# First mixer: level 0's masked copies ahead of the rotations, and two groups of TensorE's order exchanged

## Chip, cores and metric

One core of a Trainium2 chip. The metric is device time in microseconds (us). The kernel runs two transformer layers on 256 tokens of width 1024 in float32.

## What is computed

Layer 0 is a mixer followed by a mixture of experts; layer 1 is another mixer followed by another mixture of experts. The change lies in the mixer of layer 0. There one projection feeds two parts whose outputs are concatenated and projected back:

```python
def even_mixer(h, w_in, lb, hg_norm, q_norm, k_norm, w_out, pos):
    proj = h @ w_in
    hq, hf, hi, hg, aq, ak, av, iq, ik, iw = jnp.split(proj, ...)
    o_h = hgrn2_scan(hq, kk, hi, log f)          # 4 heads of 128, chunks of 64
    o_h = rmsnorm(o_h) * silu(hg)
    q, k = rope(rmsnorm(aq)), rope(rmsnorm(ak))  # 8 query heads, 2 key heads of 64
    o_a = dsa_attention(q, k, v, iq, ik, iw)     # top 64 keys by an index score, softmax
    return concat(o_h, o_a) @ w_out
```

The scan is a gated linear recurrence. The attention takes, for each query, the 64 keys with the highest index score among those of its own and earlier chunks.

## The kernel before

The tokens are two blocks of 128 (t = 0, 1). The projection's weights lie in HBM as units of at most 2 MB; SP loads them into a ring of seven slots in SBUF. The units of layer 0's mixer are, in order, index queries, forget gates, keys and values, queries, scan queries, scan inputs (unit 5) and output gates (unit 6). Units 5 and 6 are multiplied in halves: `half (5, 0)` is unit 5 for tokens 0 to 127, 16 matmuls into PSUM bank 2, and `half (5, 1)` the other 128 tokens, into bank 3; unit 6 follows in the same banks.

The scan is worked out as a masked product of decayed queries and keys, put together from nine levels. Level 0 is the diagonal. For each other level, GpSimd subtracts cumulated decays (L1218, L1219), ScalarE takes exponentials (`level` on ScalarE, L1008), VectorE multiplies them into keys and queries (`mix`, L1420 and L1421), TensorE makes 16 products (`level`, L558 and L561; 8 at level 8), and VectorE copies the part that the level's mask selects into the matrix `aT` (`take_level`, L1406). The products of levels 0 to 5 go to banks 0 and 1, so TensorE may start level v only when level v-1 has been taken (semaphore `lv_ok`).

The attention runs beside it. VectorE picks the 64 keys (`keys`), normalizes queries and keys (`norms`, L1361) and rotates them (`rotate`, L1380, which calls `rope`, L1308, once for each block of tokens; six instructions, L1314 to L1319). TensorE transposes the rotated heads (`turned`, L438), and ScalarE copies them out of PSUM (L999). Then come three batches, each with the same steps: TensorE's `score` (L521), VectorE's masked maximum (`score`, L1429), ScalarE's exponentials (`score`, L1015), TensorE's transposes (`turn`, L530), ScalarE's copies (`turn`, L1021), TensorE's `value` (L540), VectorE's division (`value`, L1441).

Each engine runs these pieces in an order that is written out by hand in three lists at the top of the file, `PE_ORDER` (L59), `DVE_ORDER` (L62) and `ACT_ORDER` (L66); a loop at the end of each engine's part (L575, L1451, L1027) calls the pieces in that order. An engine takes its instructions in order, so a piece that waits for a semaphore holds up everything behind it in its list. GpSimd works through the levels in order; it writes level v's differences when VectorE has mixed level v-2.

Behind the lists come the last products of the scan (L572), the out projection in two halves (L598), and the normalization of the scan's output on VectorE, whose last instructions (L1464) raise `on_ok`. TensorE's second part of the out projection waits for it, and so does SP: the first loads of expert weights into the extra buffers (L379, issued at L341) wait for `on_ok`. The expert weights of a layer are eight groups of twelve units of 2 MB. SP's queue is in order too: five units go into ring slots as the mixer's units leave them (slot of unit 6 after `half (6, 1)`), then come the extra buffers, then everything else.

A piece's waits are its first lines, as here for TensorE's and ScalarE's part of one batch of attention:

```python
def turn(b):                                  # TensorE
    pe.wait_ge(at_exp, b + 1)                 # ScalarE's exponentials of batch b
    ...
def value(b):                                 # TensorE
    pe.wait_ge(at_t, 2 * (b + 1))             # ScalarE's two copies of the turned batch
    ...
def half_unit(which):                         # TensorE
    ...
        pe.wait_ge(e_half, t + 1)             # unit 6: unit 5's copy out of the same bank
```

Of the kernel before, what the change touches and what calls it, by code (L numbers as in the profile page):

```python
# [55 lines left out]

BATCHES = [(0, list(range(8))), (1, [0, 1, 4, 5]), (1, [2, 3, 6, 7])]

PE_ORDER = [("half", (5, 0)), ("level", 0), ("half", (5, 1)), ("level", 1), ("turned", 0), ("level", 2), ("score", 0), ("half", (6, 0)),  # L59
            ("turn", 0), ("level", 3), ("value", 0), ("score", 1), ("half", (6, 1)), ("turn", 1), ("level", 4), ("value", 1), ("score", 2),  # L60
            ("level", 5), ("level", 6), ("turn", 2), ("level", 7), ("value", 2), ("level", 8)]
DVE_ORDER = [("keys", 0), ("keys", 1), ("norms", 0), ("query", 0), ("mix", 1), ("mix", 2), ("rope", 0), ("level", 0), ("rope", 1),  # L62
             ("level", 1), ("mix", 3), ("level", 2), ("mix", 4), ("score", 0), ("level", 3), ("mix", 5), ("value", 0), ("score", 1),
             ("level", 4), ("mix", 6), ("value", 1), ("score", 2), ("level", 5), ("mix", 7), ("level", 6), ("mix", 8), ("level", 7),
             ("value", 2), ("level", 8), ("sum", 0)]
ACT_ORDER = [("level", 1), ("level", 2), ("queries", 0), ("half", (5, 0)), ("level", 3), ("level", 4), ("half", (5, 1)), ("turned", 0),  # L66
             ("level", 5), ("score", 0), ("level", 6), ("half", (6, 0)), ("turn", 0), ("score", 1), ("level", 7), ("half", (6, 1)),
             ("turn", 1), ("score", 2), ("level", 8), ("turn", 2), ("gate", 0)]

LEVEL_BANK = (0, 0, 0, 0, 0, 0, 2, 0, 2)  # L70
# [28 lines left out]
def build(nc, A, out):  # L99
# [7 lines left out]
    with ctx:  # L107
# [3 lines left out]
        def sem(name):  # L111
            return ctx.enter_context(nc.semaphore(name))
# [157 lines left out]
        rot_ok, rot_ps, rot_t = sem("rot_ok"), sem("rot_ps"), sem("rot_t")  # L270
# [128 lines left out]
        def _(pe):  # L399
# [174 lines left out]

            for kind, n in PE_ORDER:  # L575
                {"level": level, "half": half_unit, "turned": turned, "score": score, "turn": turn, "value": value}[kind](n)
# [362 lines left out]
        def _(act):  # L939
# [86 lines left out]

            for kind, n in ACT_ORDER:  # L1027
                {"level": level, "half": half_unit, "queries": queries, "turned": turned, "score": score, "turn": turn, "gate": gate}[kind](n)
# [195 lines left out]
        def _(dve):  # L1224
# [83 lines left out]
            def rope(t, h0, h1):  # L1308

                n = h1 - h0  # L1310
                a1, a2 = rb[:, t, h0:h1, 0:32], rb[:, t, h0:h1, 32:64]
                cos, sin = bc(cs[:, t:t + 1, 0:32], [P, n, 32]), bc(cs[:, t:t + 1, 32:64], [P, n, 32])
                r = lambda m: rt[:, m, 0:32 * n].rearrange("p (h d) -> p h d", h=n)
                ch.put(tt(r(0), a1, cos, ALU.mult))  # L1314
                ch.put(tt(r(1), a2, sin, ALU.mult))
                ch.put(tt(r(2), a2, cos, ALU.mult))
                ch.link(tt(r(3), a1, sin, ALU.mult))
                ch.link(tt(a1, r(0), r(1), ALU.subtract))
                tt(a2, r(2), r(3), ALU.add).then_inc(rot_ok, 1)  # L1319
# [58 lines left out]
                    ch.link(tt(rb[:, t, 8:10, :], rb[:, t, 8:10, :], bc(qkn[:, 1:2, :], [P, 2, 64]), ALU.mult))  # L1378

            def rotate(t):  # L1380
                rope(t, 0, 10)

            def query(_):
# [66 lines left out]

            for kind, n in DVE_ORDER:  # L1451
                {"level": take_level, "mix": mix, "keys": top_keys, "norms": norms, "rope": rotate, "query": query, "score": score,
                 "value": value, "sum": hgrn_sum}[kind](n)
# [477 lines left out]
```

## Time and profile before

| | |
|---|---|
| time, median of 3 runs | 1262.14 us (1261.61 to 1263.18) |
| profiled execution | 1262.0 us, its span 1260.1 us |
| mean granted TensorE clock | 0.924 of full speed |
| busy: TensorE, VectorE, ScalarE, GpSimd | 79%, 27%, 14%, 1% |
| chain that ended last | DMA 39%, TensorE 35%, SP's queue 16% |
| read from HBM | 457 MB, mean 364 GB/s over the span |

The profile is of one execution. PE is TensorE's matmuls, PEld its weight loads, DVE VectorE, ACT ScalarE, POOL GpSimd, and SPq SP's queue of transfers. Times in a timeline count from the span's start; a line is one instruction or several of the same kind that follow each other, and a bracket at its end tells how long the engine had been idle before it and what it then waited for. The granted clock is TensorE's clock as a share of full speed (1.00 is 2.4 GHz, 0.50 is 1.2 GHz).

### The profile page before, as it was taken

The page shows a single profiled execution, that of the slowest core. Times are in us where ns is not written, and L with a number is a line of the kernel's source. Part 1 is how long each engine was busy: PE and PEld are TensorE (multiplying, and loading weights), DVE is VectorE, ACT ScalarE, POOL GpSimd, SP SyncE. Part 2 cuts the span into 40 slices and gives each one's busy share as a digit, 9 for nine tenths or more (in the row PEclk, how much of TensorE's full clock was granted, in tenths as well). Part 3 has the DMA queues.
Part 4 walks back from the last instruction along what each step waited for, and adds up shares of the span by engine and source line. Part 5 has one row for each costly group of instructions (what it writes and reads, how often), then busy time and mean ns, then how long its engine had stood idle before and what let it go on. Part 6 is the DMA issues. An engine that isn't in the chain of part 4 may idle for free.

```text
span 1260.1 us, 20742 instructions
## 1 busy us (share of the span) xinstructions
PE 1001.1 (79%) x8905; PEld 606.8 (48%) x8905; DVE 334.1 (27%) x992; ACT 178.8 (14%) x393; POOL 18.4 (1%) x20
## 2 busy tenths in 40 slices
PE   9999999757576766667999999999857576666665
PEld 6667466424242424333888775465424242423332
DVE  4895341101010110002747553241101010101001
ACT  2315130000000000001224561030000000000000
POOL 0121000000000000000000000000000000000000
PEclk9999999988887988888999999999979887989889
DMA  9931599999999999999944546679999999999998
GB/s 377 416 135 67 226 400 429 428 427 431 426 430 427 430 427 430 428 428 426 409 171 168 184 151 273 261 294 427 426 430 427 430 427 430 428 430 428 430 426 334
DMA packets 34656, 458.91 MB, mean 364 GB/s; under 512 B 3856, under 2 KB 4656, under 8 KB 7216
## 3 DMA queue, kind: packets, MB, share of 16 engines
q1 hardware_dynamic: 33408, 454.00, 86.2%
q10 hardware_dynamic: 1200, 4.23, 1.0%
q8 instruction: 36, 0.59, 0.2%
q14 instruction: 12, 0.10, 0.0%
HBM read 457.13 MB, written 1.08 MB: 364 GB/s over the span
## 4 chain that ended last, share of the span: by engine, by line
DMA 39%; PE 35%; SPq 16%; DVE 2%; issue 1%; another core or an unknown queue 0%; ACT 0%; DVEq 0%
DMA extra<-in_moe_units 20%; DMA ring<-in_moe_units 19%; SPq L341 16%; PE bank L793 11%; PE bank L685 6%; PE bank L895 4%; PE bank L704 3%; PE bank L598 2%; PE bank L664 1%; PE bank L422 1%; PE bank L716 1%; PE bank L852 1%; PE bank L561 1%; PE bank L643 1%; PE bank L630 1%
## 5 line engine op out<-in xcount | busy, mean ns | idle before, releaser
L685 PE MATMUL bank<-ring,xT 128*32 128x256 f32 x2560 | 185.3, 437 | 83.4 <-DMA ring<-in_moe_units 83.4
L685 PE MATMUL bank<-extra,xT 128*32 128x256 f32 x1536 | 123.5, 475 | 71.8 <-DMA extra<-in_moe_units 71.8
L685 PEld LDWEIGHTS bank<-ring,xT 128*32 128x32 f32 x2560 | 84.4, 119 | 169.1 <-DMA ring<-in_moe_units 96.8
L793 PE MATMUL bank<-h,ring 128*128 128x256 f32 x576 | 130.1, 382 | 0.0
L793 PEld LDWEIGHTS bank<-h,ring 128*128 128x128 f32 x576 | 107.4, 190 | 16.5 <-issue 2.9
L685 PEld LDWEIGHTS bank<-extra,xT 128*32 128x32 f32 x1536 | 53.1, 128 | 128.4 <-DMA extra<-in_moe_units 84.9
L704 PE MATMUL bank<-ring,gates_ 128*32 128x256 f32 x1024 | 73.2, 434 | 42.6 <-DMA ring<-in_moe_units 42.6
L704 PE MATMUL bank<-extra,gates_ 128*32 128x256 f32 x1024 | 71.2, 425 | 35.8 <-DMA extra<-in_moe_units 33.4
L1575 DVE TENSOR_TENSOR hT<-hT,bank 128x128 f32<-128x128 f32 x64 | 18.4, 288 | 254.6 <-ACT hT L1065 254.6
L1065 ACT ACTIVATE hT<-bank 128x128 f32<-128x128 f32 x64 | 17.7, 277 | 449.0 <-PE bank L685 449.0
L716 PE MATMUL bank<-xT,gates_ 128*128 128x256 f32 x256 | 70.2, 407 | 3.8 <-DVE xT L1580 2.2
L704 PEld LDWEIGHTS bank<-ring,gates_ 128*32 128x32 f32 x1024 | 34.0, 121 | 79.4 <-DMA ring<-in_moe_units 56.7
L1577 DVE COPY gates_<-bank 128x128 f32<-128x128 f32 x64 | 18.7, 292 | 190.9 <-PE bank L692 190.9
L704 PEld LDWEIGHTS bank<-extra,gates_ 128*32 128x32 f32 x1024 | 34.3, 119 | 64.3 <-DMA extra<-in_moe_units 41.6
L1580 DVE COPY xT<-bank 128x256 f32<-128x256 f32 x32 | 13.6, 425 | 180.7 <-PE bank L704 180.7
L664 PE MATMUL bank<-hT,xn 128*128 128x128 f32 x512 | 60.4, 276 | 1.0 <-DVE hT L1534 1.0
L716 PEld LDWEIGHTS bank<-xT,gates_ 128*128 128x128 f32 x256 | 45.8, 195 | 31.8 <-issue 21.3
L664 PEld LDWEIGHTS bank<-hT,xn 128*128 128x128 f32 x512 | 59.7, 192 | 2.7 <-issue 2.0
L1483 DVE TENSOR_TENSOR xT<-bank,small 128x512 f32<-128x512 f32 (+1 forms) x36 | 22.8, 633 | 111.6 <-PE bank L664 111.6
L1068 ACT ACTIVATE xT<-bank 128x256 f32<-128x256 f32 x32 | 12.3, 383 | 270.4 <-PE bank L704 270.4
L422 PE MATMUL bank<-ring,hT 128*128 128x512 f32 (+1 forms) x128 | 49.4, 541 | 0.0
L422 PEld LDWEIGHTS bank<-ring,hT 128*128 128x128 f32 x128 | 23.9, 190 | 22.2 <-issue 21.2
(312 smaller groups left out, 899.8 us busy)
## 6 DMA issues: line engine op xcount, KB each, us to landing
ring<-in_moe_units SPq DMA_DIRECT2D x112, 2048.0 KB, 49.1
extra<-in_moe_units SPq DMA_DIRECT2D x80, 2048.0 KB, 49.3
ring<-in_od_in_units SPq DMA_DIRECT2D x10, 2048.0 KB, 32.6
ring<-in_ev_in_units SPq DMA_DIRECT2D x5, 2048.0 KB, 26.5
ring<-in_od_out_units SPq DMA_DIRECT2D x4, 2048.0 KB, 8.1
ring<-in_ev_out_units SPq DMA_DIRECT2D x2, 2048.0 KB, 28.4
hT<-sums ACTq DMA_DIRECT2D x4, 512.0 KB, 4.4
every<-sums ACTq DMA_DIRECT2D x4, 512.0 KB, 5.6
```

The costliest lines, as they stand in the source:

```text
L341: sp.dma_start(moe_memory(layer, u), moew[layer, bass.ds(group, 1), u, :, :].rearrange("g p c -> (g p) c")) \
L422: last = mm(bank[b][:, 0:n], hT[:, k, P * t:P * t + P], w[:, k, :], start=(k == 0), stop=(k == KT - 1))
L598: last = mm(bank[2 * t + h][:, :], hT[:, 4 * OUT_BLOCKS[0][u] + k, P * t:P * t + P], w[:, k, 512 * h:512 * h + 512], start=(u == 0 and k = ...
L664: last = mm(bank[b][:, P * (k - k0):P * (k - k0) + P], xn[:, t, P * k:P * k + P], sel[:, 4 * t:4 * t + 4, :].rearrange("p e c -> p (e c)") ...
L685: last = mm(bank[4 + e % 2][32 * j:32 * j + 32, 0:256], xT[:, 4 * part + k, CAP * e:CAP * e + CAP], w[:, k, :, 256 * (j // 2) + j % 2:256 ...
L704: last = mm(bank[6 + q % 2][32 * e:32 * e + 32, 256 * (q // 2):256 * (q // 2) + 256], heT[:, e, CAP * j:CAP * j + CAP], w[:, e, j, :], sta ...
L716: last = mm(o, pgT[:, t, :], ys[:, 256 * q:256 * q + 256], start=last_quarter, stop=end and q > 0)
L793: last = mm(o, w[:, k, P * q:P * q + P], (h2 if u else hT)[:, k, :], start=(k == 0), stop=(k == KT - 1))
L895: last = mm(bank[4 * (g % 2) + 2 * t + h][:, :], yT(g, k)[:, P * t:P * t + P], w[:, k, 512 * h:512 * h + 512], start=(k == 0), stop=(k == 3))
L1483: tt(xT[:, k0:k0 + n, :], bank[b][:, 0:P * n].rearrange("p (k c) -> p k c", k=n), bc(fg[:, layer, k0:k0 + n].unsqueeze(2), [P, n, P]), ALU ...
L1575: tt(he, sg, bank[4 + e % 2][:, P:2 * P], ALU.mult).then_inc(m["he_ok"], 1)
L1577: v_.tensor_copy(heT[:, e, :], bank[7][:, 0:P]).then_inc(m["ht_ok"], 1)
```

## The change

Three orders change, and one wait is added.

- VectorE: `take_level(0)` goes ahead of `rotate(0)`, so the order is mix 2, take 0, rotation 0, rotation 1, take 1.
- TensorE: `half (6, 0)` moves from behind score 0 to behind level 1, ahead of the transposes (`turned`) and level 2; and level 3 and turn 0 change places. The order is now half (5, 1), level 1, half (6, 0), turned, level 2, score 0, level 3, turn 0, value 0.
- ScalarE: the copy of half (5, 1) goes ahead of the exponentials of levels 3 and 4, and the copy of half (6, 0) goes from behind level 6 to behind the copies of the transposes, ahead of level 5.
- VectorE's second rotation waits for the last instruction of the first, since both use the scratch tile `rt` and the copies of level 0 no longer stand between them.

No instruction is added or removed but that wait, and no transfer changes.

```diff
-PE_ORDER = [("half", (5, 0)), ("level", 0), ("half", (5, 1)), ("level", 1), ("turned", 0), ("level", 2), ("score", 0), ("half", (6, 0)),
-            ("turn", 0), ("level", 3), ("value", 0), ("score", 1), ("half", (6, 1)), ("turn", 1), ("level", 4), ("value", 1), ("score", 2),
+PE_ORDER = [("half", (5, 0)), ("level", 0), ("half", (5, 1)), ("level", 1), ("half", (6, 0)), ("turned", 0), ("level", 2), ("score", 0),
+            ("level", 3), ("turn", 0), ("value", 0), ("score", 1), ("half", (6, 1)), ("turn", 1), ("level", 4), ("value", 1), ("score", 2),
             ("level", 5), ("level", 6), ("turn", 2), ("level", 7), ("value", 2), ("level", 8)]
-DVE_ORDER = [("keys", 0), ("keys", 1), ("norms", 0), ("query", 0), ("mix", 1), ("mix", 2), ("rope", 0), ("level", 0), ("rope", 1),
+DVE_ORDER = [("keys", 0), ("keys", 1), ("norms", 0), ("query", 0), ("mix", 1), ("mix", 2), ("level", 0), ("rope", 0), ("rope", 1),
...
-ACT_ORDER = [("level", 1), ("level", 2), ("queries", 0), ("half", (5, 0)), ("level", 3), ("level", 4), ("half", (5, 1)), ("turned", 0),
-             ("level", 5), ("score", 0), ("level", 6), ("half", (6, 0)), ("turn", 0), ("score", 1), ("level", 7), ("half", (6, 1)),
+ACT_ORDER = [("level", 1), ("level", 2), ("queries", 0), ("half", (5, 0)), ("half", (5, 1)), ("level", 3), ("level", 4), ("turned", 0),
+             ("half", (6, 0)), ("level", 5), ("score", 0), ("level", 6), ("turn", 0), ("score", 1), ("level", 7), ("half", (6, 1)),
...
             def rotate(t):
+                if t:
+                    dve.wait_ge(rot_ok, 3)
                 rope(t, 0, 10)
```

## Rows read from the trace of the kernel before

**Rows 1.** The page's slices of the span, 40 of 31.5 us: DMA busy share.

```profile
DMA  9931599999999999999944546679999999999998
```

**Rows 2.** Timeline of TensorE, 50 to 150 us: start, us, engine, line, operation.

```profile
74.62 1.95 PE L558 MATMUL bank<-extra 128*128 128x128 f32 x16
76.40 7.03 PE L422 MATMUL bank<-ring,hT 128*128 128x512 f32 x16
84.11 2.02 PE L561 MATMUL bank<-xn 128*128 128x128 f32 x16 [0.68 <-DVE aT L1406]
86.80 1.31 PE L438 MATMUL bank<-con,rb 128*128 128x128 f32 x10 [0.67 <-DVE rb L1319]
88.17 2.02 PE L561 MATMUL bank<-xn 128*128 128x128 f32 x16
90.13 1.71 PE L521 MATMUL bank<-tt_ 64*128 64x128 f32 x16
91.77 7.13 PE L422 MATMUL bank<-ring,hT 128*128 128x512 f32 x16
98.74 1.04 PE L530 MATMUL bank<-con,pr 128*128 128x128 f32 x8
99.61 1.95 PE L561 MATMUL bank<-xn 128*128 128x128 f32 x16
101.40 1.90 PE L540 MATMUL bank<-av,rt 128*128 128x64 f32 x16
...
121.11 1.09 PE L530 MATMUL bank<-con,pr 128*128 128x128 f32 x8 [0.45 <-ACT pr L1015]
```

**Rows 3.** SP's timeline, and stretches: length, busy PE, PEld, DVE, ACT, POOL, PEclk, DMA share, GB/s.

```profile
139.22 1.91 SPq L341 DMA_DIRECT2D extra<-in_moe_units  x4
...
131.20:139.20 8.00, 7.15 (x17) 2.98 (x17) 7.33 (x19) 0.00 (x0) 0.00 (x0) 1.00 0.00 0
139.20:150.00 10.80, 10.80 (x32) 5.30 (x33) 0.00 (x0) 1.57 (x4) 0.00 (x0) 1.00 0.91 360
```

**Rows 4.** Timeline of VectorE, 50 to 150 us.

```profile
77.27 1.39 DVE L1314 TENSOR_TENSOR rt<-rb,extra 128x320 f32<-128x320 f32 x1
...
82.64 1.33 DVE L1406 COPY_PREDICATED aT<-extra,bank 128x512 f32<-128x512 int32 x2
84.00 0.49 DVE L1314 TENSOR_TENSOR rt<-rb,extra 128x320 f32<-128x320 f32 x1
...
86.26 0.49 DVE L1319 TENSOR_TENSOR rb<-rt 128x320 f32<-128x320 f32 x1
...
88.06 0.69 DVE L1420 TENSOR_TENSOR xn<-extra,ro 128x512 f32<-128x512 f32 x1
...
90.23 1.34 DVE L1406 COPY_PREDICATED aT<-extra,bank 128x512 f32<-128x512 int32 x2 [0.88 <-PE bank L561]
91.61 0.69 DVE L1420 TENSOR_TENSOR xn<-extra,ro 128x512 f32<-128x512 f32 x1
...
92.82 0.29 DVE L1429 CUSTOM_DVE_ANT_0 pr<-bank,sc 128x128 f32<-128x128 f32 x1
```

**Rows 5.** Timeline of ScalarE, 50 to 150 us.

```profile
87.50 1.36 ACT L999 ACTIVATE tt_<-bank 128x512 f32<-128x512 f32 x3 [3.34 <-PE bank L438]
...
95.08 0.40 ACT L1015 ACTIVATE pr<-pr,sm 128x128 f32<-128x128 f32 x1 [2.29 <-DVE sm L1432]
...
98.17 1.04 ACT L1008 ACTIVATE ro<-ro 128x1024 f32<-128x1024 f32 x1
...
99.69 1.06 ACT L1021 ACTIVATE rt<-bank 128x512 f32<-128x512 f32 x2
```

**Rows 6.** Expert loop: TensorE's timeline, and one stretch (length, PE busy, PEclk, DMA, GB/s).

```profile
252.96 2.02 PE L685 MATMUL bank<-ring,xT 128*32 128x256 f32 x32 [2.79 <-DMA ring<-in_moe_units]
257.86 3.47 PE L685 MATMUL bank<-ring,xT 128*32 128x256 f32 x32 [2.61 <-DMA ring<-in_moe_units]
...
258.00:261.00 3.00, 3.00 (x32) 0.52 0.99 421
```

## The prediction

> **What bounds the kernel now.** I read the page first, then the chain of work that ended last, then the timelines of the first mixer engine by engine. The page's DMA line shows the case's shape: transfers fill the chip for most of the span, with holes in the third and fourth slices, about 63 to 126 us [rows 1]. That hole is the part of the first mixer that the diff touches. The reader should see in TensorE's timeline that from 74.6 us on its groups stand almost shoulder to shoulder [rows 2]: it waits 0.68 us ahead of level 1, 0.67 us ahead of the head transposes ("turned"), and 0.45 us ahead of turn 2. So here TensorE's own work sets the pace, and an edit can win only those waits, or lose by opening a new one. What follows the mixer is bound by transfers that can't start earlier: SP issues four extra expert units only at 139.22, when VectorE has written the last operand of the second half of the out projection; the DMA share is 0.00 from 131.2 to 139.2 [rows 3]. All later expert loads stand behind these in SP's queue. **So a microsecond gained or lost in the mixer should arrive at the end whole.**
>
> **The change part by part.**
>
> *The masked copy of level 0 ahead of rotation 0.* VectorE's rotations began at 77.27, and the copies of level 0 came only at 82.64 [rows 4]; level 1 on TensorE waited for them and started at 84.11. Moved, the copies start at 77.3 and take 1.33 us. No row shows them beside GpSimd, which was at work then: bound it by the rotation's first multiply, 1.39 us there and 0.49 when alone [rows 4], a factor of 2.8, so 1.3 to 3.8 us. Either end (78.6, 81.1) lies under the projection half (5,1), which starts at 76.40 and holds TensorE for 6.97 (the distance from 91.77 to 98.74, the start of the next group) [rows 2]. TensorE is free at 83.37, so level 1 starts 0.74 earlier. I take the low end; it makes no difference.
>
> *The rotations.* They do the same work behind that copy and end where they ended, about 86.75 (86.26 + 0.49) [rows 4]. The added wait of rotation 1 on rotation 0 stands behind its own engine's last instruction; bounds are 0 and the spacing of about 0.5 us of one such instruction, and the later takes and mix 3 queue behind it. All of that is hidden by the next edit.
>
> *Half (6,0) moved ahead of "turned".* Level 1 takes 1.79 (99.61 to 101.40), so the half runs from 85.16 to 92.13, and the rotations' end at 86.75 no longer matters. The transposes then take 1.09 (ten of the kind of which eight take 0.87, 98.74 to 99.61), level 2 1.79, score 0 1.64 (90.13 to 91.77) [rows 2]: score 0 ends at 96.65. ScalarE's copies of the transposes end 2.06 after these start (87.50 + 1.36 against 86.80) [rows 2, 5], at 94.19, under level 2. From level 1's start to score 0's end there were 84.11 to 91.77, 7.66 us; without the half there are now 6.31. **Gain so far: 0.74 + 1.35 = 2.1 us.**
>
> *What the half used to cover.* In the kernel before, the same 6.97 us lay between score 0 and turn 0. In that time VectorE took level 2 at 90.23, did mix 4 at 91.61 and the eight score reductions from 92.82 [rows 4], and ScalarE did eight exponentials from 95.08 until 98.17 [rows 5]. TensorE started turn 0 at 98.74, without waiting. That latency doesn't shrink: take 2 needs level 2, which TensorE now runs from 93.22; its copy starts 1.9 to 2.1 later (2.06 in the trace, with a small gap at the front), say at 95.2, and 7.94 us on (90.23 to 98.17) the exponentials are done, at 103.1. Between score 0 and turn 0 there is now only level 3. It needs take 2, done at 96.55 (95.2 + 1.34), so it starts at 96.65 without loss and ends at 98.44. **TensorE then waits 4.7 us for turn 0.** Behind turn 0 stands value 0, which level 3 used to separate from it: it needs ScalarE's two copies, and on ScalarE the exponentials of level 6 (1.04) come first, then the copies (1.06) [rows 5]. So value 0 starts at about 105.2 against 101.40: a second wait of 1.1 us. Price: 4.7 + 1.1 = 5.9; with the 2.1 gained, the mixer is **3.8 us later** from value 0 on. Bounds: the distance between the score and the end of the exponentials is from one execution, and the small overlaps above are 0.1 to 0.2 each, so 3.4 to 4.2.
>
> *What stands behind.* Score 1, half (6,1), turn 1 and so on come in the old order, and all of TensorE's work is still ahead of it; only 0.45 us of waiting is left there to absorb anything [rows 2], and that wait hangs on the same chain, so it moves too. On ScalarE, the copy of half (5,1) goes ahead of the exponentials of levels 3 and 4, which wait for it until about 84; mix 3, which started at 88.06 [rows 4] behind take 1, needs the first of them, so this costs nothing (without that cover, at most the 1 us of an exponential). On SP's queue, only half (6,1) releases a ring slot among the moved or shifted groups; one 2 MB load goes out some 4 us later into the hole of [rows 1], and is not needed before the router. GpSimd's queue keeps its order.
>
> *The clock.* At present this stretch runs at a granted clock of 1.00, as the rows of the mixer's end show [rows 3]. A TensorE that stands for nearly five microseconds may lose it. The expert loop shows what happens: after 2.61 us of waiting, the granted clock of 258 to 261 was 0.52 (the 1.2 GHz level), and a group of 32 matmuls took 3.47 us where the same group took 2.02 behind a wait of 2.79 [rows 6]. So waits of this size do both, and one nearly twice as long, followed by a short group and another wait, will more likely than not be answered by a fall. One group at the low clock lost 1.45 us; a low stretch that begins in the wait loses less, one that lasts for two such groups 2.9. I take 1.9, between one and two, since value 0, score 1 and half (6,1) follow without a wait.
> The Trainium skill, "TensorE: Matmul & The Clock Gate", Part 1, says that "the default state is throttled, and activity releases the throttle"; by it the wait is followed by a low stretch, as in the row at 257.86, while the row at 252.96 shows that not every wait is. By the page the sum is 3.8 + 1.9, by the row at 252.96 it is 3.8.
>
> **Sum.** The profiled execution took 1262.0 us by its own time, with a span of 1260.1; the median of the three runs is 1262.14, 0.14 above. -2.1 + 5.9 + 1.9 = +5.7, on the median: **1267.8 us**.
>
> **The rivals.**
> - *The wait comes, but the clock holds.* For it: the wait of 2.79 that left the clock alone [rows 6]. Against: this wait is longer, with a second behind it. +3.8, 1265.9. Chance 0.17.
> - *Not slower: the delay is caught up behind the mixer.* The place is SP's queue between 139 us and the first loop over the experts; if the DMA engines had free time there, loads that go out 3.8 us late would be done at the old time. Price 0, 1262.1. It decides where the engines idle by 3.8 us more than the mixer's hole: the first stretch after 139.2 has a share of 0.91 of 10.8 us, about 1 us free [rows 3]. Against it: that 1 us is too little, and everything in that stretch, loads and products, itself waits for the mixer. Chance 0.07.
> - *Faster: the softmax is ready.* If the score reductions ended early enough for turn 0 to start at 98.44, only the gain of 2.1 would be left: 1260.0. For that take 2 through ScalarE's exponentials would need 3 us and not 7.94 [rows 4, 5]. Chance 0.04, and even this stays within 0.2% more often than not.
> - *Worse: a long low stretch.* If the clock stays low through turn 0, value 0, score 1 and most of half (6,1), or falls again at the mixer's later waits, two to four groups' worth are lost: +6.7 to +9.6, beyond 1270. Chance 0.06.
>
> **How the numbers follow.** The forecast (wait and low clock) has 0.66. Its own bounds are 3.4 + 0.9 and 4.2 + 3.7, 1266.4 to 1270.0; with the rival of the held clock the range goes down to 1264.9, and 1264.6 takes in some loss of the small overlaps. Range 1264.6 to 1270.2. It leaves out the two cases that are not slower and the worst, 0.17. About 0.2% (2.5 us) is what a measurement here can tell from no change. Faster by more than that needs more than all of TensorE's waits: 0.02. Same: 0.09, the rest of these two rivals. Slower: 0.89.
>
> **What would show each step right or wrong.** TensorE's timeline of the changed kernel should have level 1 within 0.2 us of the end of half (5,1), half (6,0) ahead of the transposes with no wait, then a wait of 4 to 5 us ahead of turn 0 put down to ScalarE's pr, and one of about 1 us ahead of value 0. VectorE's reductions of score 0 should start near 97.8. SP's four extra units should go out at about 143 to 145 instead of 139.22. The granted clock should show a stretch at half from about 102 on; if it is 1.00 throughout, the term of 1.9 is wrong. If turn 0 doesn't wait, the whole forecast falls; if SP's issue moves but the end does not, the claim that the delay arrives whole is wrong.

## The result and the profile after

The changed kernel takes **1269.45 us** (median of 5 runs, 1269.06 to 1270.08) against 1262.14: a ratio of 1.0059, with a 95% interval of 1.0048 to 1.0071. It is slower by 7.3 us, by more than the 0.2% that counts here; the forecast was 1267.8, and 1264.6 to 1270.2. The profiled execution took 1269.5 us, its span 1267.7, 7.6 more than before.

TensorE's timeline of the changed kernel, from half (5, 1) to turn 1 (columns as in [rows 2]):

```profile
76.28 7.03 PE L422 MATMUL bank<-ring,hT 128*128 128x512 f32 x16
83.15 1.95 PE L561 MATMUL bank<-xn 128*128 128x128 f32 x16
84.94 7.03 PE L422 MATMUL bank<-ring,hT 128*128 128x512 f32 x16
91.81 1.25 PE L438 MATMUL bank<-con,rb 128*128 128x128 f32 x10
92.90 1.95 PE L561 MATMUL bank<-xn 128*128 128x128 f32 x16
94.78 1.71 PE L521 MATMUL bank<-tt_ 64*128 64x128 f32 x16
96.42 2.05 PE L561 MATMUL bank<-xn 128*128 128x128 f32 x16
102.97 1.56 PE L530 MATMUL bank<-con,pr 128*128 128x128 f32 x8 [4.50 <-ACT pr L1015]
105.21 3.67 PE L540 MATMUL bank<-av,rt 128*128 128x64 f32 x16 [0.69 <-ACT rt L1021]
108.81 2.09 PE L521 MATMUL bank<-tt_ 64*128 64x256 f32 x8
110.83 8.53 PE L422 MATMUL bank<-ring,hT 128*128 128x512 f32 x16
119.20 1.04 PE L530 MATMUL bank<-con,pr 128*128 128x128 f32 x8
```

The two waits of [rows 2] ahead of level 1 and the transposes are gone. Then comes what the half used to cover: 4.50 us of idle ahead of turn 0, put down to ScalarE's exponentials, and 0.69 ahead of value 0, put down to its copies. Value 0 starts at 105.21 against 101.40. But look also at the lengths of the next three lines: value 0 takes 3.67 us where it took 1.90, and half (6, 1) 8.53 where such a group took 7.13. The clock says why; here are stretches of the same timeline (length, busy TensorE, granted clock, DMA share, GB/s):

```profile
102.00:103.00 1.00, 0.04 (x1) 1.00 0.00 0
103.00:104.00 1.00, 1.00 (x7) 0.72 0.00 0
104.00:105.00 1.00, 0.52 (x3) 0.50 0.00 0
...
112.00:113.00 1.00, 1.00 (x3) 0.50 0.00 0
113.00:114.00 1.00, 1.00 (x2) 0.66 0.00 0
114.00:115.00 1.00, 1.00 (x4) 1.00 0.00 0
```

The clock falls to its lower level (1.2 GHz) within a microsecond of TensorE's return to work and stays there for about 10 us: most of turn 0, all of value 0 and score 1, and the first 2.9 us of the half. From value 0's start to turn 1's start it was 9.87 us (101.40 to 111.27) and is now 13.99, so 4.1 us of the loss are clock, and 3.8 (105.21 against 101.40) are waits net of what was gained. A few tenths of those 3.8 are clock too, since turn 0 itself ran slowly (1.56 us, and 1.04 before). The sum stands in SP's timeline, four extra units at 147.16 instead of the 139.22 of [rows 3], 7.94 later:

```profile
147.16 1.89 SPq L341 DMA_DIRECT2D extra<-in_moe_units  x4
```

From there to the end of the span it is 1120.5 us, and 1120.9 before. The delay arrives all but whole.

VectorE's timeline of the changed kernel answers to [rows 4]:

```profile
77.11 1.33 DVE L1408 COPY_PREDICATED aT<-extra,bank 128x512 f32<-128x512 int32 x2
78.48 1.02 DVE L1314 TENSOR_TENSOR rt<-rb,extra 128x320 f32<-128x320 f32 x1
79.43 1.43 DVE L1315 TENSOR_TENSOR rt<-rb,extra 128x320 f32<-128x320 f32 x1
80.78 0.48 DVE L1316 TENSOR_TENSOR rt<-rb,extra 128x320 f32<-128x320 f32 x1
...
85.00 0.49 DVE L1319 TENSOR_TENSOR rb<-rt 128x320 f32<-128x320 f32 x1
...
94.88 1.34 DVE L1408 COPY_PREDICATED aT<-extra,bank 128x512 f32<-128x512 int32 x2 [6.81 <-PE bank L561]
96.25 0.69 DVE L1422 TENSOR_TENSOR xn<-extra,ro 128x512 f32<-128x512 f32 x1
...
97.47 0.28 DVE L1431 CUSTOM_DVE_ANT_0 pr<-bank,sc 128x128 f32<-128x128 f32 x1
```

The masked copy stands right behind mix 2, and the rotations end at 85.5 where they ended at 86.75; 0.15 us of that is only that this execution runs ahead (mix 1 starts at 73.85, before at 74.00), so they end 1.1 us earlier. Then VectorE itself is idle for 6.81 us until TensorE has done level 2: while half (6, 0) runs, the softmax that it used to cover can't even begin.

### The profile page after: what moved, and what is told of

Same layout as the page of the kernel before. It is cut to its first block, busy times and chain, and to the rows that moved or that the text cites. A ratio compares the mean times of both kernels' runs of the same rounds, so it can differ in the third digit from the quotient of the medians.

```text
span 1267.7 us, 20742 instructions
## 1 busy us (share of the span) xinstructions
PE 1006.3 (79%) x8905; PEld 609.4 (48%) x8905; DVE 332.9 (26%) x992; ACT 178.5 (14%) x393; POOL 18.1 (1%) x20
## 4 chain that ended last, share of the span: by engine, by line
PE 41%; DMA 32%; SPq 22%; DVE 2%; issue 1%; another core or an unknown queue 1%; ACT 1%; DVEq 0%
SPq L341 21%; DMA ring<-in_moe_units 16%; DMA extra<-in_moe_units 12%; PE bank L793 11%; PE bank L685 6%; PE bank L895 4%; PE bank L422 4%; DMA ring<-in_od_in_units 4%; PE bank L704 3%; PE bank L430 2%; PE bank L598 2%; PE bank L664 1%; PE bank L716 1%; DMA extra<-in_x 1%; PE bank L852 1%
## 5 line engine op out<-in xcount | busy, mean ns | idle before, releaser
L1485 DVE TENSOR_TENSOR xT<-bank,small 128x512 f32<-128x512 f32 (+1 forms) x36 | 22.8, 632 | 113.7 <-PE bank L664 113.7
```

Of the source, the lines that this page charges most:

```text
L1485: tt(xT[:, k0:k0 + n, :], bank[b][:, 0:P * n].rearrange("p (k c) -> p k c", k=n), bc(fg[:, layer, k0:k0 + n].unsqueeze(2), [P, n, P]), ALU ...
```

## The experiments

The theory after the result: VectorE's edit gains about a microsecond; half (6, 0) ahead of the transposes uncovers the chain from score 0 to turn 0; the loss is that wait, and the low clock that follows it. Rivals: the exchange of level 3 and turn 0 carries the loss; the groups behind the wait are slow for another reason than the clock; VectorE's edit costs something that the half hides. The first four kernels take the change apart; ScalarE's part was not run by itself.

**VectorE's part alone** (`dve_only`): TensorE's and ScalarE's orders as before.

```diff
-PE_ORDER = [..., ("level", 1), ("half", (6, 0)), ("turned", 0), ("level", 2), ("score", 0), ("level", 3), ("turn", 0), ...
+PE_ORDER = [..., ("level", 1), ("turned", 0), ("level", 2), ("score", 0), ("half", (6, 0)), ("turn", 0), ("level", 3), ...
```

(the minus line is the changed kernel's, here and below)

> VectorE's part of the change alone, TensorE and ScalarE in the old order. Theory (the order on TensorE costs the time, VectorE's edit alone gains): level 1 starts at about 83.2 us and doesn't wait, the rotations end near 85.4 and the transposes follow with a wait of 0.5; turn 0 doesn't wait. Gain 0.8 to 1.4 us: 1260.8 to 1261.4, SP's four extra units at about 138. Rival (the copies beside GpSimd or the added wait cost something that the changed kernel hides under half (6,0)): 1262.1 or above.

Measured: 1260.65 us, a ratio of 0.9990 to before (0.9981 to 0.9999). TensorE's timeline:

```profile
76.83 7.03 PE L422 MATMUL bank<-ring,hT 128*128 128x512 f32 x16
83.70 1.95 PE L561 MATMUL bank<-xn 128*128 128x128 f32 x16
86.14 1.31 PE L438 MATMUL bank<-con,rb 128*128 128x128 f32 x10 [0.50 <-DVE rb L1319]
...
98.07 1.04 PE L530 MATMUL bank<-con,pr 128*128 128x128 f32 x8
```

This execution ran 0.43 us later from the start, so distances are compared: from half (5, 1)'s start to SP's four extra units it takes 61.72 us, and 62.82 before. The wait ahead of level 1 is gone, that ahead of the transposes is 0.50 instead of 0.67, and turn 0 doesn't wait. The transposes start 9.31 us after half (5, 1) instead of 10.40. VectorE's edit gains 1.1 us by itself, 1.3 by the medians; the rival falls.

**The exchange alone** (`exchange_only`): VectorE's part, and level 3 ahead of turn 0, the half in its old place, ScalarE's order as before.

```diff
-PE_ORDER = [..., ("level", 1), ("half", (6, 0)), ("turned", 0), ("level", 2), ("score", 0), ("level", 3), ("turn", 0), ...
+PE_ORDER = [..., ("level", 1), ("turned", 0), ("level", 2), ("score", 0), ("half", (6, 0)), ("level", 3), ("turn", 0), ...
```

> VectorE's part, and level 3 ahead of turn 0 on TensorE, with half (6,0) left between score 0 and turn 0. Theory: turn 0 finds its exponentials ready, but value 0 stands right behind turn 0 and waits about 0.9 us for ScalarE's copies; no fall of the clock. About 0.9 above the run with VectorE's part alone: 1261.7 to 1262.3. Rival (the exchange carries a good part of the loss of 7.3 us): 1264 or above.

Measured: 1261.76, ratio 1.0001 (0.9992 to 1.0010). The distance to SP's units is 62.69, 0.97 more than with VectorE's part alone, and TensorE's timeline has the reason:

```profile
99.47 1.04 PE L530 MATMUL bank<-con,pr 128*128 128x128 f32 x8
101.24 2.00 PE L540 MATMUL bank<-av,rt 128*128 128x64 f32 x16 [0.74 <-ACT rt L1021]
```

and ScalarE's:

```profile
97.12 1.04 ACT L1008 ACTIVATE ro<-ro 128x1024 f32<-128x1024 f32 x1
...
100.11 1.08 ACT L1021 ACTIVATE rt<-bank 128x512 f32<-128x512 f32 x2 [1.37 <-PE bank L530]
```

With nothing between turn 0 and value 0, the copies show, and give back what VectorE's edit gained. They wait for turn 0 alone here: the exponentials of level 6 (at 97.12) are done before turn 0 starts. The exchange alone is worth a microsecond, not seven.

**The half alone** (`half_only`): level 3 back behind turn 0, the half ahead of the transposes.

```diff
-            ("level", 3), ("turn", 0), ("value", 0), ("score", 1), ...
+            ("turn", 0), ("level", 3), ("value", 0), ("score", 1), ...
```

> The changed kernel with level 3 back behind turn 0, so half (6,0) ahead of the transposes is what is left of TensorE's edits. Theory (moving the half uncovers the softmax): turn 0 starts at about 103 as in the changed kernel, behind a wait of 6.3 us instead of 4.5, level 3 covers ScalarE's copies, and the clock falls; value 0 is 0.4 to 2 us later than in the changed kernel: 1269.8 to 1271.5. Rival (the exchange carries the loss): 1266 or below.

Measured: 1268.27, ratio 1.0054 (1.0038 to 1.0069). So moving the half does the damage. But the number lies below the range, and under the changed kernel. TensorE's timeline, then stretches of it:

```profile
102.98 1.97 PE L530 MATMUL bank<-con,pr 128*128 128x128 f32 x8 [6.49 <-ACT pr L1015]
104.74 3.25 PE L561 MATMUL bank<-xn 128*128 128x128 f32 x16
107.82 1.90 PE L540 MATMUL bank<-av,rt 128*128 128x64 f32 x16
```

```profile
100.00:101.00 1.00, 0.00 (x0) 0.81 0.00 0
101.00:102.00 1.00, 0.00 (x0) 0.50 0.00 0
...
107.00:108.00 1.00, 1.00 (x10) 0.77 0.00 0
108.00:109.00 1.00, 1.00 (x12) 1.00 0.00 0
```

Turn 0 starts where it did, behind the longer wait that was expected. The clock, though, falls in the middle of the wait, so that part of the low stretch passes while TensorE has nothing to do, and it is back at 107.5, not 113.7. Value 0 starts 2.6 us later than in the changed kernel (107.82), later than was expected, but from there to turn 1 it is 9.87 us again, as before the change. What the clock costs depends on how much of the low stretch falls on work.

**The wait filled** (`fill`): work for TensorE ahead of turn 0. The kernel's own `turnover(b, n)` issues n matmuls on constants into PSUM bank b.

```diff
             for kind, n in PE_ORDER:
+                if (kind, n) == ("turn", 0):
+                    turnover(7, 20)
```

> The changed kernel with 20 bfloat16 matmuls of 128x512 into the unused PSUM bank 7 between level 3 and turn 0 (about 4.3 us of work whose results nobody reads). Theory (the loss is a wait of 3.8 us net plus 4.1 us of low clock behind it): turn 0 and value 0 start where they did, about 103 and 105, the granted clock stays 1.00, value 0, score 1 and half (6,1) take 1.8, 1.1 and 7.0 us: 1265.2 to 1265.8. Rival (the groups behind the wait are slow for another reason than the clock, or the clock falls whatever TensorE does there): 1269 or above.

Measured: 1265.60, ratio 1.0029 (1.0017 to 1.0041). Of the 7.3 us, half has come back, with nothing useful added. TensorE's timeline:

```profile
98.62 4.26 PE L405 MATMUL bank<-ones 128*128 128x512 bf16 x19
103.07 1.09 PE L530 MATMUL bank<-con,pr 128*128 128x128 f32 x8 [0.18 <-ACT pr L1017]
104.97 2.00 PE L540 MATMUL bank<-av,rt 128*128 128x64 f32 x16 [0.81 <-ACT rt L1023]
106.90 1.14 PE L521 MATMUL bank<-tt_ 64*128 64x256 f32 x8
107.97 7.13 PE L422 MATMUL bank<-ring,hT 128*128 128x512 f32 x16
```

Turn 0 and value 0 start where they did, and the groups behind them are as short as before the change; the granted clock is 1.00 from 98 to 118. So the two terms are shown apart: the wait costs 3.7 us net (SP's distance 66.52 against 62.82), the clock the rest, 4.4 (70.88 in the changed kernel against 66.52).

**The half alone, with the wait filled** (`half_fill`): the edit of half_only, and `turnover(7, 28)` ahead of turn 0.

> The changed kernel with level 3 back behind turn 0 (as in half_only) and 28 bfloat16 matmuls of 128x512 into the unused PSUM bank 7 ahead of turn 0, about 6 us of work that nobody reads. It tells what the exchange of level 3 and turn 0 is worth when the clock stays. Theory (the exchange shortens TensorE's way by 0.7 us, since level 3 runs in the wait, and half_only came out faster only because its low stretch of the clock lay better): clock 1.00, turn 0 at 103.0, value 0 at 105.6 to 105.7, 1266.0 to 1266.6, that is 0.5 to 1 above fill. Rival (the exchange costs time of its own by the second wait): at or below fill's 1265.6 by over 0.5, 1265.1 or less.

Measured: 1267.78, ratio 1.0048 (1.0033 to 1.0063), above the expected 1266.6. TensorE's timeline of the profiled execution, which took 1266.28:

```profile
102.94 1.09 PE L530 MATMUL bank<-con,pr 128*128 128x128 f32 x8 [0.33 <-ACT pr L1017]
...
105.66 1.90 PE L540 MATMUL bank<-av,rt 128*128 128x64 f32 x16
```

In it the clock stays at 1.00, and value 0 starts at 105.66, as expected; SP's distance is 67.22, 0.70 above fill. With the clock held, the exchange of level 3 and turn 0 gains 0.7 us, because level 3 runs inside the wait; half_only came out faster than the changed kernel through the place of its low stretch, which cost 2.1 us (69.36 against 67.22) and not 4.4. The times don't show it: four executions fell in two pairs, 1265.6 and 1266.3, and 1269.3 and 1269.4. The profile is of one of the lower pair, what the other two did 3 us longer isn't known, and the conclusion rests on the trace.

**The softmax begun earlier** (`score_first`): if turn 0 waits for the chain through VectorE, a shorter chain must show.

```diff
-             ("level", 1), ("mix", 3), ("level", 2), ("mix", 4), ("score", 0), ("level", 3), ...
+             ("level", 1), ("mix", 3), ("score", 0), ("level", 2), ("mix", 4), ("level", 3), ...
-             ("half", (6, 0)), ("level", 5), ("score", 0), ("level", 6), ("turn", 0), ("score", 1), ...
+             ("half", (6, 0)), ("level", 5), ("score", 0), ("turn", 0), ("level", 6), ("score", 1), ...
```

> The changed kernel with VectorE's score reductions of batch 0 ahead of take 2 and mix 4, and ScalarE's copies of turn 0 ahead of the exponentials of level 6. Theory (turn 0 waits for the chain score 0, reductions, exponentials, and VectorE's place in it can be had back): reductions at 96.6 instead of 97.5, exponentials done at 101.9, turn 0 at 102.0; level 3 then waits for take 2 until about 100.1. The clock falls all the same. Value 0 at 104.0 to 104.5 instead of 105.2: 1267.0 to 1268.8. Rival (the wait ahead of turn 0 is set by something else): 1269.5, turn 0 at 103.

Measured: 1265.80, ratio 1.0031 (1.0018 to 1.0044), less than expected. TensorE's timeline:

```profile
94.91 1.71 PE L521 MATMUL bank<-tt_ 64*128 64x128 f32 x16
100.02 3.75 PE L561 MATMUL bank<-xn 128*128 128x128 f32 x16 [3.40 <-DVE aT L1408]
103.57 1.92 PE L530 MATMUL bank<-con,pr 128*128 128x128 f32 x8
106.17 2.00 PE L540 MATMUL bank<-av,rt 128*128 128x64 f32 x16 [0.69 <-ACT rt L1021]
```

The wait moved ahead of level 3, where take 2 is late now, and turn 0 waits for nothing: ScalarE starts its exponentials at 98.68 instead of 99.72. So VectorE's place in the chain is part of the wait. The clock fell at 98.6, early in the wait, and was back at 105.5, so level 3 and turn 0 paid for it and value 0 did not. Value 0 is later than expected (106.17), because level 3 and turn 0 ran at the low clock (3.75 and 1.92 us), which the expectation had left out; the time is shorter all the same, since value 0, score 1 and the half run at full speed.

**The changed kernel again** (`again`), for where the low stretch lies in another execution.

> The changed kernel once more, for where the low stretch of the clock lies in another profiled execution. If wait and low stretch are tied to the order of TensorE's work, the fall comes within 1 us of 103.3 and the stretch is 10 us long again, value 0 near 105.2, score 1 near 108.8, about 1269.5. If the low stretch falls by chance anywhere in and behind the wait, this profile shows another start or length (6 to 10 us), with SP's four units 1 to 3 us earlier and 1266.5 to 1268.5.

Measured: 1270.46, ratio 1.0066 (1.0050 to 1.0083). Stretches of its timeline:

```profile
103.00:104.00 1.00, 1.00 (x5) 0.55 0.00 0
...
112.00:113.00 1.00, 1.00 (x2) 0.50 0.00 0
113.00:114.00 1.00, 1.00 (x3) 0.82 0.00 0
```

The fall comes 0.3 us earlier and the stretch is as long; SP's distance is 70.87 against 70.88. Two profiles of the same kernel agree; the next run shows that this doesn't settle where the stretch falls.

**The second wait filled** (`fill_second`): is it the short wait ahead of value 0 that keeps the clock low for 10 us and not 7? (The added wait lets VectorE's reductions of score 0 finish, which read bank 4.)

```diff
             for kind, n in PE_ORDER:
+                if (kind, n) == ("value", 0):
+                    pe.wait_ge(at_max, 1)
+                    turnover(4, 2)
```

> The changed kernel with two bfloat16 matmuls of 128x512 into the unused PSUM bank 4 between turn 0 and value 0, where TensorE waited 0.69 us; the wait of 4.5 ahead of turn 0 stays. Theory (the first wait alone brings the clock down): the fall near 103.3 as in the changed kernel, value 0 near 105.3. If the second wait is what keeps the clock low for 10 us instead of 7, the stretch ends about 3 us earlier and half (6,1) runs at full speed: 1267.7 to 1268.3. If the first wait alone sets the length, 1269.3 to 1269.8.

Inconclusive. The profiled execution took 1270.65 us; in it the clock is low from 101.4 to 115, over 13 us, longer than without the filling:

```profile
101.00:102.00 1.00, 0.00 (x0) 0.70 0.00 0
...
114.00:115.00 1.00, 1.00 (x3) 0.50 0.00 0
```

Up to turn 0 TensorE does here what it does in the changed kernel, at the same times (turn 0 at 102.98 behind a wait of 4.51), and yet the clock fell 2 us earlier, inside the wait. So the place of the fall differs between executions with the same work ahead of it. The four executions spread from 1266.05 to 1270.65 (median 1268.56, ratio 1.0046, 1.0029 to 1.0063). So the second wait isn't shown to lengthen the stretch, and what makes it 7 us in one profile and 10 or 13 in another stays open.

**A version ahead of both** (`split`): one of the half's eight products ahead of the transposes, seven behind score 0, on top of dve_only.

```diff
             def turned(_):
+                loaded(0, 6)
+                pe.wait_ge(e_half, 1)
+                rows_half(6, 0, 2, range(1))
```

> dve_only with one of the eight products of half (6,0) (0.87 us) ahead of the transposes and the other seven where the half stood. Theory (the half covers both the rotations' end and the softmax, so only as much as fills the wait ahead of the transposes may move): no wait ahead of the transposes, turn 0 right behind its exponentials with at most 0.1 us of wait, SP's four extra units about 0.5 us earlier than in dve_only, 1260.0 to 1260.4. Rival (what is moved ahead is missing behind score 0 at once): no gain over dve_only's 1260.65, turn 0 waits by 0.4 or more.

Measured: 1260.52, ratio 0.9990 (0.9981 to 0.9999). Like dve_only it is faster than the kernel before by an interval that just leaves out 1, and by time the two can't be told apart. In the profile the wait ahead of the transposes is gone, but turn 0 waits 0.28, and SP's distance is 61.35, 0.37 less than dve_only's. Between the expectation and its rival: 0.87 us of the half is already slightly more than the softmax can spare.

The profiled executions of before, changed and six of the runs side by side; the distance is from half (5, 1)'s start to SP's extra units, the last column the low clock between 98 and 118 us:

| kernel | half (6, 0) | level 3 | distance, us | low clock |
|---|---|---|---|---|
| before | behind score 0 | behind turn 0 | 62.82 | none |
| dve_only | behind score 0 | behind turn 0 | 61.72 | none |
| exchange_only | behind score 0 | ahead of turn 0 | 62.69 | none |
| fill | ahead, wait filled | ahead of turn 0 | 66.52 | none |
| half_fill | ahead, wait filled | behind turn 0 | 67.22 | none |
| score_first | ahead | ahead of turn 0 | 67.68 | 98.6 to 105.5 |
| half_only | ahead | behind turn 0 | 69.36 | 100.6 to 107.5 |
| changed | ahead | ahead of turn 0 | 70.88 | 103.4 to 113.7 |

Behind SP's units, all eleven profiles take between 1120.4 and 1122.1 us to the end of the span; of a difference in time, up to 1.7 us can come from there.

## Why the prediction was right, and where it was off

The forecast's mechanism held: a wait of 4.5 us ahead of turn 0 and a second one ahead of value 0, with a fall of the clock behind them. The time lies in the range, 1.65 us above the forecast. But the sum had the waits somewhat too long and the clock at less than half of what it cost, and its sign for SP's units, 143 to 145, was missed by 2 us (147.16).

- **VectorE's copy moved, and the two waits won.** Forecast 2.1 us until score 0's end; measured, the distance from half (5, 1)'s start to the end of score 0 is 20.14 (76.28 to 96.42, level 3's start) with the half in it, and was 15.37 (76.40 to 91.77) without: 20.14 - 6.87 is 13.27, 2.1 less. Right. That the rotations would end where they had was wrong by 1.1 us, to their good, and it was covered as argued; in dve_only it shows, since there the transposes start 1.1 us earlier.
- **The wait ahead of turn 0, and the one ahead of value 0.** Forecast 4.7 and 1.1; measured 4.50 and 0.69, with turn 0 itself longer by the low clock. Value 0 was forecast at 105.2 and started at 105.21, which is luck: the waits were 0.6 us shorter, and the slow turn 0 took nearly as much longer. (By the prediction's own rows the second wait is 1.2, as its sum of 5.9 has it.) The fill shows these waits as a term of their own, 3.7 us net against the 3.8 of the sum.
- **The clock.** The step that was mis-sized. It took 1.9 us, "between one and two" groups' worth. In the changed kernel the stretch began only as work resumed and lasted 10 us, so it cost 4.1 by the groups from value 0 on and 4.4 by the fill. What came is nearer to the rival with a long low stretch, through turn 0, value 0, score 1 and into half (6, 1), which had a chance of 0.06: the 7.3 us lie within its +6.7 to +9.6. (That rival says "beyond 1270", but 6.7 on the median is 1268.8.) So the time came out inside the range because the range was wide, up to 1270.0, and not because the term was right. (Its lower end of 1264.9 doesn't follow either: the shortest wait, 3.4, gives 1265.5.) The row with a wait of 2.61 and the low clock after it [rows 6] was the right one to go by for the sign, but the stretch there lasted 3.4 us, and here three times that. The Trainium skill, "TensorE: Matmul & The Clock Gate", Part 1, has a low default state that activity lifts; the trace agrees in kind, down behind a wait of 4.50 us and up again under work.
- **The delay arrives whole.** 7.94 us at SP's units, 7.6 at the end of the span, 7.3 between the medians. The rival of a delay caught up behind the mixer is worth at most 0.3 to 0.6 us, not 3.8, and that lies within the spread of what follows SP's units. The prediction counted 0.45 us of waiting that could absorb something; TensorE has two more waits there, both for VectorE's work on the scan's output, and the three are as long after the change (0.46, 0.78 and 0.81 us) as before it (0.45, 0.78 and 0.81), so they absorbed nothing.
- **ScalarE's exponentials of level 6 ahead of the copies** were put at a microsecond of the second wait. They cost next to nothing: in fill, where the clock is held, the wait is 0.81, and in exchange_only, where they are done before turn 0 starts, it is 0.74. The wait comes from the copies standing right behind turn 0. In the changed kernel the later copy waits for turn 0, slowed by the clock, and not for level 6.

## What to carry to other kernels

When a long independent group is moved to fill a short wait, look at what it covered where it stood: here 7 us of matmuls hid the 6.5 us from the score products to their softmax, and were spent on waits of 1.4. Here a wait of several microseconds on TensorE had to be priced with the low clock behind it, which cost 2.1 to 4.4 us by the part of the low stretch that fell on work; filling the wait with matmuls that nobody reads brought back half of the 7.3 us, though covering it with real work is worth more (dve_only, where the half stays in its place: 1260.65 against 1265.60). An edit of three orders is best run in parts: the one on VectorE was a gain by itself.

## What the runs showed of the hardware

The masked copy was not slowed beside GpSimd: 1.33 us at 77.11, as long as at 82.64 [rows 4], although GpSimd was at work from 75.2 to 80.5, while the rotation's first two multiplies behind it took 1.02 and 1.43, and the third 0.48 once GpSimd had finished. The prediction had bounded the copy at 3.8. Before, three multiplies ran beside GpSimd (1.39, 1.33 and 1.43 us); with one slowed multiply fewer, VectorE came out 1.1 us ahead. The Trainium skill, "SBUF — State Buffer", section "SBUF: two separate sides", names instructions with two SBUF inputs as those that contend with GpSimd; the trace agrees, for the multiply has two such inputs, while the copy has its mask in SBUF and takes its data from PSUM. It is one place in one kernel; no run moved the copy to test it.

The clock fell inside the wait in three profiles (at 98.6 in score_first, 100.6 in half_only, 101.4 in fill_second) and just behind it in the two of the changed kernel (103.4 and 103.1), and it stayed low from 7 to over 13 us. The two profiles of the changed kernel agreed within half a microsecond, fill_second with the same work ahead of the fall did not; what sets the place and the length is not shown.
